# Inverse roots of the norms by logarithm and exponential on ScalarE, and latents ahead of angles in the first pass

## The reference, cut to what matters

```python
def rms_norm(x, g):                      # query latent (512), key/value latent (256), and 128 in the second layer
    xf = x.astype(jnp.float32)
    inv = lax.rsqrt(jnp.mean(xf * xf, axis=-1, keepdims=True) + RMS_EPS)
    return (xf * inv).astype(x.dtype) * g

def layer_norm(x, g, b):                 # behind each layer, over 1024 features
    mu = jnp.mean(xf, axis=-1, keepdims=True)
    var = jnp.mean(jnp.square(xf - mu), axis=-1, keepdims=True)
    return ((xf - mu) * lax.rsqrt(var + LN_EPS)).astype(x.dtype) * g + b
...
kv = (rms_norm(x_kv, kv_norm_g) @ w_ukv)         # keys without angle, values
k_rope = apply_rope(k_rope_raw, cos, sin)        # keys with angle, from positions
```

## Time and profile before

| what | value |
|---|---|
| median of three runs | 3543.56 us |
| the profiled execution: time | 3533.97 us |
| the profiled execution: first to last instruction | 3532.0 us |
| PE, DVE, ACT, POOL busy | 94%, 59%, 38%, 20% |
| granted TensorE clock, mean | 0.969 |
| chain that ended last | PE 78%, DVE 10%, ACT 6%, issue 5% |

### The profile page before, as it was taken

One profiled execution on the slowest core, in us unless ns is written; L12 is line 12 of the kernel. 1 busy time (PEld: TensorE's weight loads), 2 busy tenths in 40 slices (PEclk: granted clock), 3 DMA queues, 4 the chain that ended last, 5 costly groups with the idle time before them and its releaser, 6 DMA issues.

```text
span 3532.0 us, 49781 instructions
## 1 busy us (share of the span) xinstructions
PE 3319.1 (94%) x18464; PEld 2044.8 (58%) x18464; DVE 2066.5 (59%) x4970; ACT 1358.4 (38%) x2595; POOL 706.4 (20%) x1093
## 2 busy tenths in 40 slices
PE   8999999999999999999989999899998898998887
PEld 3444577567656755745567455674555673545656
DVE  4417734773475457435563587835768635878653
ACT  2212312222222313132341465515775514786552
POOL 0016032112101210111121101312351111352011
PEclk9999999999999999989989999999999999998999
DMA  5226135304501420341204211041210041110004
GB/s 192 72 66 245 49 113 167 114 13 125 161 2 50 148 78 1 91 159 54 63 25 146 71 61 33 25 143 60 66 45 1 25 152 54 51 57 1 1 3 129
DMA packets 114159, 275.22 MB, mean 78 GB/s; under 512 B 11096, under 2 KB 12672, under 8 KB 111872
## 3 DMA queue, kind: packets, MB, share of 16 engines
q1 hardware_dynamic: 105584, 256.31, 22.8%
q10 hardware_dynamic: 8336, 15.74, 1.3%
HBM read 239.75 MB, written 32.26 MB: 77 GB/s over the span
## 4 chain that ended last, share of the span: by engine, by line
PE 78%; DVE 10%; ACT 6%; issue 5%; POOL 1%; DMA 0%; SPq 0%; ACTq 0%; DVEq 0%; POOLq 0%
PE bank L2342 24%; PE bank L2356 17%; PE o_acc L2514 6%; PE bank L2497 6%; PE bank L2744 3%; PE bank L2631 3%; PE bank L2504 3%; PE bank L2663 3%; PE bank L2756 2%; PE o_acc L2770 2%; PE bank L2593 1%; ACT prob_t L1485 1%; DVE tmp L2048 1%; PE bank L2415 1%; ACT index L1628 1%
## 5 line engine op out<-in xcount | busy, mean ns | idle before, releaser
L2342 PE MATMUL bank<-group_even,weights 128*128 128x512 f32 x1152 | 507.6, 598 | 11.2 <-DMA group_even<-in_x_t 5.8
L2342 PE MATMUL bank<-group_odd,weights 128*128 128x512 f32 x960 | 426.7, 600 | 6.2 <-ACT tmp L1471 6.2
L2342 PEld LDWEIGHTS bank<-group_even,weights 128*128 128x128 f32 x1152 | 218.4, 192 | 275.5 <-issue 275.3
L1430 ACT ACTIVATE probs<-probs,stat 128x512 f32<-128x512 f32 x256 | 181.7, 711 | 431.6 <-DVE stat L1747 431.6
L2342 PEld LDWEIGHTS bank<-group_odd,weights 128*128 128x128 f32 x960 | 181.9, 192 | 225.6 <-issue 225.2
L2514 PEld LDWEIGHTS o_acc<-lat,val 128*128 128x128 f32 x2048 | 242.2, 197 | 49.4 <-issue 41.4
L2514 PE MATMUL o_acc<-lat,val 128*128 128x128 f32 x2048 | 251.7, 283 | 12.9 <-DVE lat L1876 12.9
L2497 PE MATMUL bank<-k_nope,q_nope 128*32 128x512 f32 x2048 | 233.0, 595 | 0.0
L1862 DVE CUSTOM_DVE_ANT_0 probs<-bank,mask 128x512 f32<-128x512 f32 x256 | 161.4, 686 | 98.4 <-PE bank L2504 98.4
L2744 PE MATMUL bank<-kh,qa 64*128 64x512 f32 (+3 forms) x816 | 171.1, 501 | 16.0 <-DVE o_sb L2300 7.5
L1876 DVE STREAM_TRANSPOSE lat<-probs 128x512 f32<-128x512 f32 x256 | 168.8, 695 | 20.1 <-ACT probs L1430 20.0
(11 more groups left out here) (472 smaller groups left out, 6159.3 us busy)
## 6 DMA issues: line engine op xcount, KB each, us to landing
weights<-in_w_in SPq DMA_DIRECT2D x101, 512.0 KB, 3.6
weights<-w_sums SPq DMA_DIRECT2D x200, 256.0 KB, 3.3
weights<-in_w_out SPq DMA_DIRECT2D x96, 256.0 KB, 3.7
weights<-in_w_in_q SPq DMA_DIRECT2D x28, 512.0 KB, 3.6
weights<-in_w_in_q SPq DMA_DIRECT2D x54, 256.0 KB, 3.3
w_sums<-group_odd SPq DMA_DIRECT2D x10, 1024.0 KB, 4.6
weights<-in_w_i SPq DMA_DIRECT2D x20, 512.0 KB, 3.6
group_odd<-in_x_t SPq DMA_DIRECT2D x8, 1024.0 KB, 8.5
```

Source lines behind the costliest of these rows:

```text
L1430: A_(p, p, ACT.Exp, scale=QK_DIM ** -0.5, bias=stat[:, 16 + PARTS * (n % 2) + r:17 + PARTS * (n % 2) + r], accum_out=sums_1[:, i % 2, PART ...
L2342: ins = M(bank(*name)[:], ring[n % SLOTS][:, k * P:(k + 1) * P], rhs[:, k, :], start=(k == 0), stop=(k == chunks - 1))
```

## The change

It replaces each of the 20 wide roots (square root on ACT, reciprocal on DVE) by a logarithm and an exponential with scale -0.5 on ACT, so that `std` itself holds the inverse root. The small root of the meta latents (L1441) and the roots of the heads stay square roots with a reciprocal; ahead of a heads' root stands a new square root of one column into a spare column of `stat`. The semaphore `std_read` is kept for the meta root alone; elsewhere ACT waits for the product that read `std` (`scaled`, `c_normed`), and that wait stands behind the wait for the tile.

In the first pass the angle work goes behind the latents: DVE takes the raw angle keys out of PSUM first (into the buffer of `q_rope`, `raw_keys`), scales the latents, copies `k_nope`, and only then converts positions (group 0), makes the angles, waits for the sines and rotates. On ACT `rope_tables` goes behind the `v` copies. In the second pass `c_sq` goes from behind level 7 to behind level 6, ahead of the third `gate_h`, and its product stays behind level 7 as a step of its own (`c_norm`). In the query stage DVE's product of the norm goes behind the next `added` step.

Cut to its core (numbers are lines before and after):

```diff
@@ -219,0 +220,2 @@
+        if pair == 0 and lev == len(LEVELS):
+            yield ("c_sq", g)
@@ -223 +225 @@
-        yield ("c_sq", g)
+        yield ("c_norm", g)
...
@@ -932 +935 @@
-        def normalise(tag, g, dve, step, V):
+        def normalise(tag, g, dve, V):
@@ -937,6 +940 @@
-            if tag == "1":
-                step(dve, V.reciprocal(rstd, std))
-            else:
-                V.reciprocal(rstd, std).then_inc(std_read, 1)
-                dve.wait_ge(std_read, N_STD[g] + 1)
-            V.tensor_tensor(x_t[:], x_t[:], rstd.unsqueeze(1).broadcast_to([P, KC, TB]), ALU.mult).then_inc(scaled, 1)
+            V.tensor_tensor(x_t[:], x_t[:], std.unsqueeze(1).broadcast_to([P, KC, TB]), ALU.mult).then_inc(scaled, 1)
...
@@ -1317 +1305,2 @@
-                drains(A_(std, bank(*name)[:], ACT.Sqrt, scale=1.0 / width, bias=eps[:, e:e + 1]), *name)
+                step(act, A_(std, bank(*name)[:], ACT.Ln, scale=1.0 / width, bias=eps[:, e:e + 1]))
+                drains(A_(std, std, ACT.Exp, scale=-0.5), *name)
@@ -1329 +1317,0 @@
-                rope_tables(g)
@@ -1336,0 +1325 @@
+                rope_tables(g)
@@ -1505,0 +1495 @@
+                A_(spare, eps[:, 0:1], ACT.Sqrt)
@@ -1542,2 +1532 @@
-                        act.wait_ge(std_read, N_STD[g - 1])
-                        root(st, D, 1)
+                        root(st, D, 1, (c_normed, g + 1))
@@ -1563,3 +1552 @@
-                        wait_tile(act, *st)
-                        act.wait_ge(std_read, C_STD[g])
-                        drains(A_(std, bank(*st)[:], ACT.Sqrt, scale=1.0 / P, bias=eps[:, 0:1]), *st)
+                        root(st, P, 0, (scaled, G + g))
@@ -1644,2 +1631 @@
-            act.wait_ge(std_read, N_STD[G - 1])
-            root(("2var", G - 1), D, 1)
+            root(("2var", G - 1), D, 1, (c_normed, G + 1))
@@ -1693 +1679,4 @@
-            def rotate_keys(g):
+            raw = q_rope[:, :, :].rearrange("p h t -> p (h t)").rearrange("p (a t) -> p a t", a=2)
+            low, high = slice(0, ROPE), slice(ROPE, P)
+
+            def raw_keys(g):
@@ -1697,3 +1686,5 @@
-                low, high = slice(0, ROPE), slice(ROPE, P)
-                step(dve, V.tensor_copy(tmp[low, 0, :], both[high, :]))
-                drains(V.tensor_tensor(tmp[low, 1, :], both[low, :], tmp[low, 0, :], ALU.add), "krope", g)
+                step(dve, V.tensor_copy(raw[low, 0, :], both[high, :]))
+                drains(V.tensor_tensor(raw[low, 1, :], both[low, :], raw[low, 0, :], ALU.add), "krope", g)
+
+            def rotate_keys(g):
+
@@ -1703,2 +1694,2 @@
-                    step(dve, V.tensor_tensor(o_sb[to * ROPE // 2:(to + 1) * ROPE // 2, :], tmp[of, 1, :], sin[of, :], ALU.mult))
-                step(dve, V.tensor_tensor(tmp[low, 0, :], tmp[low, 1, :], cos[low, :], ALU.mult))
+                    step(dve, V.tensor_tensor(o_sb[to * ROPE // 2:(to + 1) * ROPE // 2, :], raw[of, 1, :], sin[of, :], ALU.mult))
+                step(dve, V.tensor_tensor(tmp[low, 0, :], raw[low, 1, :], cos[low, :], ALU.mult))
@@ -1711,7 +1702,10 @@
-            dve.wait_ge(vec_here, 16)
-            dve.wait_ge(const_here, 16 * 7)
-            step(dve, V.tensor_copy(pos_k[:], pos_i))
-            step(dve, V.tensor_copy(pos_q[:], pos_qi))
-            step(dve, V.tensor_copy(pos_k4, pos_k4_i))
-            for c in range(PARTS):
-                step(dve, V.tensor_reduce(same[:, c * QUAD:(c + 1) * QUAD], ident[:].rearrange("p (c n) -> p n c", n=QUAD), AX.X, ALU.add))
+            def positions():
+
+                dve.wait_ge(vec_here, 16)
+                dve.wait_ge(const_here, 16 * 7)
+                step(dve, V.tensor_copy(pos_k[:], pos_i))
+                step(dve, V.tensor_copy(pos_q[:], pos_qi))
+                step(dve, V.tensor_copy(pos_k4, pos_k4_i))
+                for c in range(PARTS):
+                    step(dve, V.tensor_reduce(same[:, c * QUAD:(c + 1) * QUAD], ident[:].rearrange("p (c n) -> p n c", n=QUAD), AX.X, ALU.add))
+
@@ -1719 +1713 @@
-                rope_args(g, g)
+                raw_keys(g)
@@ -1723,3 +1716 @@
-                V.tensor_tensor(kv_lat, kv_lat, wide(rstd, 2), ALU.mult).then_inc(k_normed, 1)
-                dve.wait_ge(rope_made, g + 1)
-                rotate_keys(g)
+                V.tensor_tensor(kv_lat, kv_lat, wide(std, 2), ALU.mult).then_inc(k_normed, 1)
@@ -1728,0 +1720,5 @@
+                if g == 0:
+                    positions()
+                rope_args(g, g)
+                dve.wait_ge(rope_made, g + 1)
+                rotate_keys(g)
@@ -1750,5 +1745,0 @@
-            def inverse_query_root(g):
-
-                wait_drained(dve, "q_sq", g)
-                step(dve, V.reciprocal(rstd, std))
-
@@ -1757 +1748,2 @@
-                V.tensor_tensor(lat[:], lat[:], wide(rstd, 4), ALU.mult).then_inc(q_normed, 1)
+                wait_drained(dve, "q_sq", g)
+                V.tensor_tensor(lat[:], lat[:], wide(std, 4), ALU.mult).then_inc(q_normed, 1)
@@ -1790,3 +1781,0 @@
-                wait_drained(dve, "1var", g - 1)
-                dve.wait_ge(centred, g)
-                step(dve, V.reciprocal(rstd, std))
@@ -1794 +1783 @@
-                V.tensor_tensor(x_of(g - 1)[:], x_of(g - 1)[:], rstd.unsqueeze(1).broadcast_to([P, KC, TB]), ALU.mult).then_inc(scaled, 1)
+                normalise("1", g - 1, dve, V)
@@ -1800 +1788,0 @@
-                inverse_query_root(g)
...
@@ -2145,5 +2132,3 @@
-                    elif kind == "c_sq":
-                        wait_drained(dve, *st)
-                        V.reciprocal(rstd, std).then_inc(std_read, 1)
-                        dve.wait_ge(std_read, C_STD[g] + 1)
-                        V.tensor_tensor(c_g, c_g, rstd, ALU.mult).then_inc(c_normed, 1)
+                    elif kind == "c_norm":
+                        wait_drained(dve, "c_sq", g)
+                        V.tensor_tensor(c_g, c_g, std, ALU.mult).then_inc(c_normed, 1)
@@ -2317,2 +2301,0 @@
-            V.reciprocal(rstd, std).then_inc(std_read, 1)
-            dve.wait_ge(std_read, N_STD[G - 1] + 1)
@@ -2320 +2303 @@
-                V.tensor_tensor(x_t[:, c, :], x_t[:, c, :], rstd, ALU.mult).then_inc(tail_scaled, 1)
+                V.tensor_tensor(x_t[:, c, :], x_t[:, c, :], std, ALU.mult).then_inc(tail_scaled, 1)
```

More of the change, by code:

```diff
@@ L257, in held @@
     st, after = plain[n], plain[n + 1]
-    return any(a[0] == "c_sq" or (a[0] == "level" and a[2] == 0 and a[3] == len(LEVELS)) for a in (st, after)) \
+    return any(a[0] in ("c_sq", "c_norm") or (a[0] == "level" and a[2] == 0 and a[3] == len(LEVELS)) for a in (st, after)) \
         or (st[0] == "level" and st[2] == 0 and st[3] == len(LEVELS) - 1)
@@ L302, in tiles_of @@
         return [("index", BG * g + step[2], step[3], h) for h in range(HI)]
-    if kind in ("2square", "2scale", "2store", "begun", "range", "bracket", "round", "ranked", "h_inverse", "h_square"):
+    if kind in ("2square", "2scale", "2store", "begun", "range", "bracket", "round", "ranked", "h_inverse", "h_square", "c_norm"):
         return []
@@ L582, in program @@
         stat = alloc(ctx, "stat", [P, 64])
+        spare = stat[:, 60:61]
         one = ExitStack()
@@ L963, in level_no @@
             return (2 * g + pair) * (len(LEVELS) + 2) + k
[L965 to L973, removed]
         def halved(ap, w):
@@ L1748, in bias_of, with scale_queries @@
                                     ALU.min).then_inc(row_max, 1)
-            def inverse_query_root(g):
+            def scale_queries(g):
                 wait_drained(dve, "q_sq", g)
-                step(dve, V.reciprocal(rstd, std))
-            def scale_queries(g):
-                V.tensor_tensor(lat[:], lat[:], wide(rstd, 4), ALU.mult).then_inc(q_normed, 1)
+                V.tensor_tensor(lat[:], lat[:], wide(std, 4), ALU.mult).then_inc(q_normed, 1)
             def pool_window(g, j):
@@ L1953, in _ @@
             V.tensor_tensor(me, me, mk, ALU.mult).then_inc(lev_diff_meta, 1)
-            normalise("1", G - 1, dve, step, V)
+            normalise("1", G - 1, dve, V)
             wait_tile(dve, "m_u")
@@ L2131, in _ @@
                     elif kind == "2scale":
-                        normalise("2", st[1], dve, step, V)
+                        normalise("2", st[1], dve, V)
                     elif kind == "f" and st[2] % 2 == 1:
```

## The result

The kernel after takes 3506.5 us (median of four runs, 3503.2 to 3508.2), the kernel before 3542.8 (3536.8 to 3544.8): a ratio of 0.990, 95% interval 0.988 to 0.992, or 36.3 us less. The profiled executions are 25.8 us apart (3532.0 and 3506.2 us of span). The forecast was 3514.7, from a gain of 28.9. Two executions of the kernel before, of 3936 and 12320 us at granted clocks of 0.83 and 0.42, are in a slower state and are left out of every comparison.

What follows compares the result with a forecast made beforehand. PE, busy 94% of the span, bounds the kernel, leaving 213 us idle as ceiling. Terms -10.3 - 8.8 - 4.8 - 2.0 - 1.3 - 2.7 + 1.0 = -28.9, applied to the median 3543.56, give 3514.7 us; range 3500 to 3530.

Steps and rivals of the forecast that it cites:

- clock terms: Matmuls running slow behind PE's pauses regain speed: 3.0 us at the first pass's start, 2.0 behind the `2scale` stalls.
- Start: First pass: latents scaled before PE needs them, so its 7.26 us wait and 3.0 of slow clock go, -10.3 us.
- `c_sq`: Second pass, ahead of `v2`: root finished behind level 6, DVE only multiplies behind level 7; -8.8 us over four groups.
- `2scale`: PE's stalls behind ACT and DVE shrink: -1.4, -1.7, -1.7 in groups 1 to 3, -4.8 us, and -2.0 of clock.
- small root: New one-column square root ahead of the heads' root brings no table earlier; 0.2 us at five places, +1.0 us.
- Price of the exponential's table: At each wide root on ACT, the exponential behind the logarithm needs its own table load, 1.28 us.
- rival (a): One table serves logarithm and exponential, no second load at any root: 4.7 us more gain, 3510.0 us; chance 0.25.
- Query stage: ACT's later root stays within 0.8 us of cover and DVE's reciprocal lies under PE, so no gain or loss: 0.
- rival (b): Bisection rounds on ACT and DVE take back gains behind `c_sq` and `2scale`: only -13.3 us, 3530.3; chance 0.20.
- Meta: Meta tokens: the exponential's own 1.28 us load, inside PE's 2.5 us wait, goes or moves under the projection; -1.3 us.
- Tail: After PE has finished: load to product shrinks from 5.40 us to 2.7, a gain of 2.7 us.
- Rival (c): ACT becomes the bound at the roots with 43.2 us more work, slower at up to 3573.5 us; chance 0.05.

Runs made afterwards that it cites:

- run 9: The kernel after, unchanged, timed again and profiled a second time: 3506.1 us, ratio 0.9885 to the kernel before.
- Run 7: The kernel after with the first pass's old order, positions and angles ahead of the latents: 3517.9 us, ratio 0.9928 to the kernel before.
- runs 1 and 5: The kernel after with wide roots by square root and reciprocal again: 3537.2 us; the same with the query stage's two reciprocals at their old places: 3528.2 us.
- Runs 11 and 12: The kernels before and after, each with 12 rounds of bisection in place of 24: 3507.3 and 3464.2 us.
- Run 3: The kernel after with one ScalarE function, `Abs_reciprocal_sqrt`, per wide root in place of logarithm and exponential: 3499.8 us, ratio 0.9879 to the kernel before.
- Run 8: The kernel after without the small one-column square root ahead of the heads' root: 3503.7 us, ratio 0.9897 to the kernel before.
- run 6: The kernel after with `c_sq` behind level 7 again, root still by logarithm and exponential: 3515.6 us, ratio 0.9922 to the kernel before.

## Why the prediction was right, and where it was off

The forecast won, from the mechanism it named, and its sum was 7 us short (28.9 for 36.3). Split the sum into waits and clock. Its clock terms were 3.0 at the start, 1.0 at `c_sq` and 2.0 at `2scale`, together 6.0; the rest is 22.9 us of PE's idle time. The profiles show 22.1 in the first pair and 215.3 - 193.2 = 22.1 in the second (each kernel's own idle time moved by 2.4 between its two profiles, so take it as 22 within some us). **The waits were right as a sum; the term that was mis-sized is the clock**, 36.3 - 22.1 = 14 us (8 to 20 by the interval) instead of 6. That the sum of the waits came within 1 us is in part luck: `c_sq` was put 3 us too high and its excess was made up by the small root, put at a loss of 1.0 that did not come, and by `2scale`, 0.7 too low; another 0.6 us of gain has no place that I could name.

The 14 are a difference, not a reading: no timed execution lists its idle time. They are supported by the mean granted clock that each execution lists: 0.9665 over 39 of the kernel before, 0.9723 over 9 of the kernel after. Against full clock that is (1 - 0.9665) x 3541 = 119 us and (1 - 0.9723) x 3505 = 97 us, 21 apart as an upper bound (slow stretches in which PE stands cost nothing). The two profiled executions had 0.969 and 0.972, 110 and 98, only 11 apart. The 10 us between 21 and 11 match the 10 by which the timed gain exceeds the profiled one.

Two other readings put the clock's part at 10 us, inside the 8 to 20. A straight line through the 39 executions gives 1.7 us of time for 0.001 of clock, not 3.5, and the 0.0058 between the means are then 10 us. And PE's busy time for the same 18464 matmuls is 3319.1 to 3325.5 us, 3322.6 in the mean, in the five profiles with reciprocals and all rounds, and 3308.7 to 3315.4, 3312.5 in the mean, in the seven with the new roots. At the places that I had named, the first pair of profiles shows 3.0, 1.0 and some 1 us, no more than my 6.0. Where the rest of the clock's part falls, and why it came with the change, no run shows.

So the execution I worked from had been granted a better clock than most, and I applied its difference to a median 9.6 us above it without asking what made up those 9.6.

How such a difference arises is seen where the change does nothing. Timeline of PE in the last attention, kernel before:

```profile
3370.71 1.09 PE L2756 MATMUL bank<-ident,index 128*128 128x128 f32 x8 [1.46 <-ACT index L1628]
3372.59 1.09 PE L2756 MATMUL bank<-ident,index 128*128 128x128 f32 x8 [0.79 <-ACT index L1628]
3373.61 1.99 PE L2744 MATMUL bank<-kh,qa 64*128 64x512 f32 x8
```

and the same instructions in the kernel after:

```profile
3340.71 1.09 PE L2739 MATMUL bank<-ident,index 128*128 128x128 f32 x8 [1.46 <-ACT index L1615]
3342.59 1.97 PE L2739 MATMUL bank<-ident,index 128*128 128x128 f32 x8 [0.79 <-ACT index L1615]
3344.49 3.79 PE L2727 MATMUL bank<-kh,qa 64*128 64x512 f32 x8
```

The same two pauses, and only one of the executions falls to the lower level behind them; the second profile of the kernel after does not either (run 9). The granted clock of the 120 us around it (stretches of time; the number behind POOL's is the clock), before and then after:

```profile
3360.00:3480.00 120.00, 107.17 (x909) 81.37 (x908) 55.31 (x182) 50.96 (x80) 14.10 (x13) 1.00 0.20 63
```

```profile
3330.00:3450.00 120.00, 107.18 (x873) 79.45 (x872) 53.04 (x177) 51.65 (x80) 13.47 (x12) 0.93 0.16 54
```

0.07 of 120 us are up to 8 us. They tell nothing of the change: the second profile of before has 0.97 there and the second of after 0.96, so the clock scatters as much between two executions of one kernel.

Step by step:
- **Start (-10.3): right.** 34.38 with no wait, and `v` at 41.25 instead of 51.32, 10.1 us earlier. Run 7 puts it at 11.4. The clock's 3.0 vary: in the second profile of before the wait was 6.95 us and the 16 matmuls behind it took 8.58, so 1.5.
- **Price of the exponential's table (1.28): right**, 20 times of 20, and rival (a) is false in this kernel. The Trainium skill ("ScalarE: Activation LUTs", "Table sets: the hidden batching unit") has the two functions in one set and counts one load for the pair; this trace disagrees, with a load of 1283 ns between each pair. That they could share one if another set were loaded is not excluded by any run. My reason for the price was too wide, though: "the load that stands ahead of every function that differs from the one before it" is not what the trace shows. Behind the exponential at 29.72 the square (L1289) and the scaled copy (L1299) start at 34.58 and 35.21 with no load.
- **Query stage (0): right as a number, wrong in its reason.** "DVE's reciprocal in this stage lies under PE" holds only at its old place; runs 1 and 5 show some 9 us hanging on the places of two reciprocals, each moved by one `added` step.
- **`c_sq` (-8.8, of it 7.8 waits): too high as waits, by the step "the gain there is what ACT's round chain moves".** The 10.9 us went whole, but 4.7 + 2.3 + 0.5 came back at `state`, `probs` and `roots`, with 1.1 gained at the heads: some 4.5 (3.5 in the second pair). Runs 11 and 12 show the rounds as the cause of 4 to 5 us of it, so rival (b) held in part; but its sign was named at the wrong step, for the waits for the heads' inverse roots hardly moved (6.6 to 5.5, and 6.6 to 6.8), while those for `state` grew.
- **`2scale` (-4.8 of waits): too low; 1.4 + 1.7 + 3.4 = 6.5, less a new wait of 1.0.** Its clock (-2.0) was too high: the matmuls behind the three waits take 0.3, -0.2 and 1.0 us less. Group 3 was the failed term. There DVE comes to the reciprocal 6.6 us after the root is ready (kernel before: root 2924.40 + 0.69, reciprocal at 2931.68), so the later root costs nothing and the whole 3.35 are won. I had charged ACT's 1.7 there as in group 2. Run 3 agrees: a root shorter by 1.97 moves group 2's wait and not group 3's.
- **Meta (-1.3): right**, 2.5 to 1.1, for the reason given (run 3 brings the 2.5 back). **Tail (-2.7): right**, 5.5 to 2.7.
- **Small root (+1.0): not seen.** Run 8 shows no less idle time without it.
- Rival (c) did not decide, but it exists: 1.5 us for `roots` in the kernel after, and the 9 us of run 6.

These places sum to 7.3 + 4.5 + 5.5 + 1.4 + 2.8 = 21.5 of the 22.1 us, and in the second pair to 6.9 + 3.5 + 5.5 + 1.4 + 2.8 = 20.1.

What stays open: part of run 7's loss, whether the one function is truly faster than the kernel after, and why the clock's part is 10 us or more when the touched steps show 5.

## What to carry to other kernels

Sum waits and clock apart: the idle time (span less PE's busy time) held the forecast's waits to 1 us (in part by luck), while the spans' difference missed the timed gain by 10. Before a profile's sum is applied to a median, compare the mean granted clock of that execution with the others'. A step that "lies under" the bound engine does so at its place in its engine's order: moved by one step, two reciprocals that had been free cost 9 us. And a move and a shorter chain can each be worth little alone: the place of `c_sq` was worth nothing with the reciprocal and 9 us with the longer root on ACT.

## What the hardware showed that was not expected

The clock's fall is not a function of the pauses alone: after the same pauses of 1.46 and 0.79 us it fell in one execution of the kernel after and not in another, and 39 executions of one kernel spread from 0.964 to 0.971 in mean clock, 3534.5 to 3549.3 us. An exponential on a tile takes 630 ns, and a logarithm or square root that reads a PSUM bank and takes its bias from a column takes 687. The bank is not what makes it longer: a plain copy of that size out of a bank (L1324) takes 597, and one with its scale from a column (L1299) 687. The square root of one column costs 202 ns.
